# A mixed-branch transformer on one core: the attention branch's units ordered by pair of heads, the products with the values issued for two heads together

## What is computed

```python
def attend(q, k, v):
    s = jnp.einsum('bqhd,bkhd->bhqk', q, k).astype(jnp.float32) * (MLA_NOPE + MLA_ROPE) ** -0.5
    p = jax.nn.softmax(s, axis=-1).astype(v.dtype)
    return jnp.einsum('bhqk,bkhd->bqhd', p, v)
...
    att_x = blocked_attend(q_x, jnp.concatenate([k_c, k_x], axis=1),
                           jnp.concatenate([v_c, v_x], axis=1)).reshape(B, T, MLA_WIDTH)
...
    att_c = attend(q_c, k_c, v_c).reshape(B, q_c.shape[1], MLA_WIDTH)
```

## Time and profile before

| | |
|---|---|
| median of 3 runs | 2821.28 us (2813.89 to 2821.5) |
| the profiled execution | 2820.24 us |
| its span, first to last instruction | 2818.4 us |
| TensorE busy | 2530.0 us, 90% |
| VectorE busy | 836.7 us, 30% |
| ScalarE busy | 595.1 us, 21% |
| loop over the units, layer 0 | 120.4 to 183.4 us |
| loop over the units, layer 1 | 1686.4 to 1725.8 us |
| granted TensorE clock in both loops | 1.00 of full speed |

### The profile page before, as it was taken

One profiled execution on the slowest core, in us unless ns is written; L12 is line 12 of the kernel. 1 busy time (PEld: TensorE's weight loads), 2 busy tenths in 40 slices (PEclk: granted clock), 3 DMA queues, 4 the chain that ended last, 5 costly groups with the idle time before them and its releaser, 6 DMA issues.

```text
span 2818.4 us, 38407 instructions
## 1 busy us (share of the span) xinstructions
PE 2530.0 (90%) x15744; PEld 1415.6 (50%) x15744; DVE 836.7 (30%) x1978; ACT 595.1 (21%) x1176; POOL 170.2 (6%) x178
## 2 busy tenths in 40 slices
PE   8999988999997999899899599978999798788875
PEld 3466367744445444344344356757888533333333
DVE  1354355311116231111111624455411521111114
ACT  4344122120002011111111143332211111111111
POOL 0000000000000111111111000000000011111110
PEclk9999989999996899999999799999999799999997
DMA  7101032411104499999897631112331699999993
GB/s 317 66 1 38 30 121 95 189 78 60 60 1 179 151 366 423 401 409 408 364 409 300 268 140 45 60 65 87 147 146 39 265 384 425 422 417 416 415 399 151
DMA packets 74703, 617.37 MB, mean 219 GB/s; under 512 B 17694, under 2 KB 17822, under 8 KB 32160
## 3 DMA queue, kind: packets, MB, share of 16 engines
q1 hardware_dynamic: 50336, 564.52, 49.0%
q0 software_dynamic: 24192, 50.39, 4.7%
HBM read 604.87 MB, written 47.71 MB: 232 GB/s over the span
## 4 chain that ended last, share of the span: by engine, by line
PE 83%; DVE 6%; issue 4%; DMA 4%; ACT 2%; SPq 0%; POOLq 0%; ACTq 0%; DVEq 0%; POOL 0%
PE bank L1828 21%; PE bank L1843 10%; PE bank L1313 9%; PE bank L300 6%; PE bank L1328 3%; PE bank L1318 3%; PE bank L1818 3%; PE bank L391 3%; PE bank L1022 2%; PE bank L1037 1%; PE bank L485 1%; PE bank L467 1%; DVE arena L2067 1%; DMA ring<-in_wexp 1%; PE bank L317 1%
## 5 line engine op out<-in xcount | busy, mean ns | idle before, releaser
L1828 PE MATMUL bank<-ring,arena 128*64 128x512 f32 (+1 forms) x1648 | 588.7, 623 | 100.4 <-issue 94.2
L1828 PEld LDWEIGHTS bank<-ring,arena 128*64 128x64 f32 (+1 forms) x1648 | 204.1, 156 | 423.8 <-issue 422.7
L1828 PE MATMUL bank<-branches,arena 128*64 128x512 f32 (+1 forms) x528 | 265.3, 661 | 0.0
L1313 PE MATMUL bank<-normed,ring 128*128 128x512 f32 (+1 forms) x768 | 255.5, 486 | 0.0
L2006 DVE TENSOR_TENSOR arena<-bank,arena 128x256 f32<-128x256 f32 x83 | 35.3, 425 | 705.5 <-ACT arena L1930 705.5
L1752 POOL DMA_INDIRECT arena<-hidden_rows,block_slots x81 | 82.2, 1015 | 2208.6 <-DVE block_slots L1580 1599.3
L1313 PEld LDWEIGHTS bank<-normed,ring 128*128 128x128 f32 x768 | 146.1, 190 | 101.6 <-issue 91.8
L1930 ACT ACTIVATE arena<-bank 128x256 f32<-128x256 f32 x83 | 31.9, 384 | 687.7 <-PE bank L1828 687.7
L300 PE MATMUL bank<-normed,ring 128*128 128x512 f32 (+1 forms) x448 | 173.9, 548 | 0.0
L1843 PE MATMUL bank<-ring,arena 128*64 128x512 f32 (+1 forms) x560 | 163.4, 597 | 1.3 <-DVE arena L2012 1.3
L1843 PE MATMUL bank<-arena 128*64 128x512 f32 (+1 forms) x528 | 141.6, 611 | 1.1 <-ACT arena L1933 1.1
(11 more groups left out here) (434 smaller groups left out, 3468.0 us busy)
## 6 DMA issues: line engine op xcount, KB each, us to landing
ring<-in_wexp SPq DMA_DIRECT2D x96, 2048.0 KB, 19.4
ring<-in_wst SPq DMA_DIRECT2D x54, 2048.0 KB, 8.3
branches<-in_wexp SPq DMA_DIRECT2D x34, 2048.0 KB, 21.0
ring<-in_wexp SPq DMA_DIRECT2D x66, 1024.0 KB, 21.3
arena<-in_wexp SPq DMA_DIRECT2D x64, 1024.0 KB, 22.3
arena<-expert_rows SPq DMA_DIRECT2D x9, 2048.0 KB, 9.9
ring<-in_wst SPq DMA_DIRECT2D x4, 1536.0 KB, 11.4
branches<-expert_rows SPq DMA_DIRECT2D x3, 2048.0 KB, 16.2
```

Source lines behind the costliest of these rows:

```text
L1313: last = nc.tensor.matmul(ps[2 * (n % 4)][:, c0:], wg[:, k, i * P:(i + 1) * P], H[:, k, c0:], start=(k == 0), stop=(k == KD - 1))
L1828: last = nc.tensor.matmul(ps[2 + s][r0:r1, :], XT_[:, s, k * P + r0:k * P + r1], wt[:, k, :], start=(k == 0), stop=(k == KD - 1))
```

## The change

It does four things. The units are ordered by pair of heads: for each pair all query blocks, and for each block the even head and then the odd one. `weigh` is called for every second unit and does both heads of a block: key tile by key tile, first the product of the even head on one half of the columns, then that of the odd head on the other. `PT` has four buffers instead of two. And the waits follow: weigh waits for the copies of both units, the copy of unit u for the weigh of unit u − 4, and the wait for a free output bank stands at the first call of each pair.

```diff
-        Pb, PT = arena(0, 4, 512), arena(2048, 2, 512)
+        Pb, PT = arena(0, 4, 512), arena(2048, 4, 512)
...
-            return [(h, q, 2 if q < 2 else 4) for h in range(HEADS) for q in range(4) if l == 0 or q >= 2]
+            return [(h, q, 2 if q < 2 else 4) for pair in range(HEADS // 2) for q in range(4) if l == 0 or q >= 2
+                    for h in (2 * pair, 2 * pair + 1)]
...
             def weigh(u):
                 h, q, nk = units[u]
-                pe.wait_ge(mla["pte"], l * MLA["pte"] + u + 1)
-                if h % 2 == 0 and h >= 4 and q == units[0][1]:
+                pe.wait_ge(mla["pte"], l * MLA["pte"] + u + 2)
+                if h >= 4 and q == units[0][1]:
                     pe.wait_ge(mla["oe"], l * MLA["oe"] + h // 2 - 1)
                 for k in range(nk):
-                    last = nc.tensor.matmul(ps[h // 2 % 2][64 * (h % 2):64 * (h % 2) + 64, q * P:(q + 1) * P],
-                                            vtok[:, k, h * DV:(h + 1) * DV], PT[:, u % 2, k * P:(k + 1) * P],
-                                            start=(k == 0), stop=(k == nk - 1))
-                last.then_inc(mla["o"], 1)
+                    for odd in range(2):
+                        last = nc.tensor.matmul(ps[h // 2 % 2][64 * odd:64 * odd + 64, q * P:(q + 1) * P],
+                                                vtok[:, k, (h + odd) * DV:(h + odd + 1) * DV], PT[:, (u + odd) % 4, k * P:(k + 1) * P],
+                                                start=(k == 0), stop=(k == nk - 1))
+                        if k == nk - 1:
+                            last.then_inc(mla["o"], 1)
...
                 flip(u)
-                if u >= 2:
-                    weigh(u - 2)
+                if u % 2 and u >= 3:
+                    weigh(u - 3)
             weigh(U - 2)
-            weigh(U - 1)
...
-                if u >= 2:
-                    act.wait_ge(mla["o"], l * MLA["o"] + u - 1)
-                nc.scalar.activation(PT[:, u % 2, 0:nk * P], ps[FLIP_BANK[u % 2]][:, 0:nk * P], ACT.Copy).then_inc(mla["pte"], 1)
+                if u >= 4:
+                    act.wait_ge(mla["o"], l * MLA["o"] + u - 3)
+                nc.scalar.activation(PT[:, u % 4, 0:nk * P], ps[FLIP_BANK[u % 2]][:, 0:nk * P], ACT.Copy).then_inc(mla["pte"], 1)
```

## The result

The changed kernel takes 2794.81 us (median of 6 runs, 2790.3 to 2801.57) against 2820.04 us for the kernel before in as many runs. The ratio is 0.9917, with a 95% interval of 0.9903 to 0.9931: 0.8% or 25 us faster. The forecast was 2799 us within 2792 to 2808.

What follows compares the result with a forecast made beforehand. TensorE was taken to bound the stage. Removed calls give 25.5 us, less 0.5 for slower steps and 0.7, 1.6 and 1.0 in fill and ends: 21.7, say 22; 2821.3 − 22 = 2799 us, range 2792 to 2808.

Steps and rivals of the forecast that it cites:

- Side by side: In weigh, both column halves run at once: a call for two heads costs what one head's call did.
- Passages: In weigh, going from full-width to half-width weights and back costs 0.34 us; 24 such passages go, 8.2 us.
- Losses: Fill and ends of the loops: 0.7 and 1.6 us lost in layer 0, 1.0 in layer 1; slower steps 0.5.
- (b): End of layer 0's loop: gain 1.6 us where three removed calls count 3.2, so 1.6 us lost.
- (a): Fill of layer 0's loop: four two-tile scores leave TensorE 0.86 us less before the first flip; 0.7 us lost.
- The copy of the pair's output: VectorE's pair_out waits for its pair's last weigh: 2.1 us to the next flip but one, TensorE has 2.1.
- The way to the end: Behind the stage: TensorE goes on at once, later waits only for the experts' loads, which move forward too.
- 24 groups of 16: Sign in the trace: weigh for two heads shows 24 groups of 16 instructions, each in about 1.1 us.
- Latency: Rival, 7%: each of 16 two-tile units stands another 0.5 us, so 8 us go; 2807 us.
- Turns: Rival, 4%: in weigh, halves take turns at 128 columns, leaving a gain of 5 us; 2816 us.
- Exposed loads: Rival, 3%: in weigh, every change of half exposes a weight load; 11 us slower, 2832 us.
- Given back later: Rival, 4%: expert stages wait for memory as before, and a shifted start could fall worse; 2821 us.

Runs made afterwards that it cites:

- passages-only kernel: Against the kernel before: four buffers, head-by-head order kept, weigh called for two units of one head; loops 57.89 and 37.39 us, ratio 0.9979.
- image first: Against the changed kernel: the image's query blocks (four key tiles) first in each pair of heads; loops 49.12 and 30.87 us, whole 2790.04 us (one run).
- four units a call: Against the changed kernel: eight buffers, weigh for two query blocks of a pair of heads; loops 46.69 and 30.09 us, ratio to before 0.9909.
- vector-slack kernel: Against the changed kernel: one more VectorE copy of 128x256 ahead of every scaling; loops 49.17 and 31.55 us, whole 2797.78 us (one run).

## Why the prediction was right

*Side by side.* Right, and cleaner than put: I took 0.5 us off for 160 steps at 3 ns, and the 16 instructions take 1.09 us, as eight did. Against the passages-only kernel it gives 16.3 us. The comparison with the experts' product carried over from 512 moving columns to 128. By the Trainium skill's rule on weight loads ("TensorE: Matmul & The Clock Gate", Part 3), a load overlaps only with matmuls of another row group; here every load takes all 128 rows, and 16 of them with their matmuls fit into 1.09 us, so the trace does not agree.

*Passages.* 0.34 us each was right in the body: 5.02 − 4.68. In total they give 7.1 instead of 8.2 us. In layer 0 that is 15 of them and not 16, since the last calls stood together before, too. In layer 1 it is 7 and not 8, and a wait of 0.52 us before the last flip comes on top.

*Losses.* In layer 1 the total was right: 9.7 expected without loss, 8.5 measured, 1.2 lost where I had 1.2. That is partly luck: the 0.2 for slower steps did not come, and the end took 6.66 us (1694.28 − 1687.62) where I had 6.55. In layer 0 I had 2.6, and 1.0 was lost (15.84 − 14.87). Of the difference, 0.3 are slower steps that did not come. The term most mis-sized is (b), the end. Its times were right (6.12 us from the last score, 6.25 said), but I set the gain of 1.6 against three full calls, and so compared ends with different work: the new end flips four tiles in units 28 and 29 where the old one flips two, 0.44 us of transposes that are missing elsewhere. And (a), the fill, left out that the old loop stood as well, before its third flip:

```profile
125.06 0.66 PE L476 MATMUL bank<-consts,arena 128*128 128x128 f32 x4 [0.32 <-DVE arena L583]
```

The new one doesn't. By the places themselves: 0.6 in the fill (the first flip comes 2.38 us after the first score, with 0.86 us less of scores between them; before it came 2.65 after), 0.34 for one passage that the old end had spared and the new one hasn't, 0.40 of idle time as printed, less 0.32: 1.0. By the starts the last two are 0.62 and 0.49, and the sum is 1.1.

*The copy of the pair's output.* "Nothing lost, but no reserve" was right. In the changed kernel TensorE never stands there. With image first, where shorter scores lie behind the copy, it stands each time, and so it does with four units a call.

*The way to the end.* Right: the loops' 23.4 us arrive, within what can be measured: 25.2 by the medians, where the runs of one kernel lie 11 to 17 us apart. The sum of 21.7 was 1.7 us short of the loops, all but 0.1 of it the loss set too high in layer 0. One wait for a load was overlooked: the experts' loads are not the only ones that TensorE waits for behind the stage. At the start of layer 1's attention branch (L391) it stands 6.3 us for weights of the projections, and 5.6 in the changed kernel. Had their load not moved forward with the rest, this wait would have taken back part of layer 0's gain.

*A slip in the signs.* There are 16 calls with 16 instructions in the two layers, and 8 with 8, where the prediction speaks of 24 groups of 16. Its sums had this right.

*Rivals.* Latency: of what the vector-slack kernel adds in layer 0, an eighth reaches the loop, in layer 1 a seventh. Turns: 16 would have to take 1.96 us. Exposed loads: they would have taken longer than 1.96. Given back later: the stages behind take what they took, but for the third branch, which moves with the clock.

What was not tried: the two products on halves with a clock below full speed, the four buffers without the new order and the order without them, and whether TensorE looks ahead for more than four instructions in other mixtures.

## What to carry to other kernels

Where products use half of the array's columns, put those for the other half in between, one by one: issued side by side, two cost here what one does. Grouping calls of one shape also saves the passage between full-width and half-width weights, here 0.34 us a time, until the next engine's rhythm shows, as it did behind the copy that waits for the longer call. And count an end or a fill by what stands idle in it, in the old kernel as in the new one, and not by what a shorter end saves, since units of other sizes move into it.

## What the runs showed of the hardware

- Matmuls with weights of 64 columns on one half of the array and then on the other take the time of one half, at 128 moving columns (16 in 1.09 us, as 8 on one half) as at 512 (32 in 7.09 us, as 16 full-width ones in 7.03).
- TensorE takes up work for the free half from behind four waiting instructions, not from behind eight: 8 issued head after head take 0.67 us, 16 take 1.58, and 1.09 when they alternate.
- A passage from full-width to half-width weights and back costs 0.34 us in a dense stream: two units take 5.02 us with two of them and 4.68 with one.
- The same kernel's third branch took 213.9 and 223.5 us in two profiles, at a mean granted clock of 0.93 and 0.89. A gain of 7 us in one pair of profiles can be just that.
